# Plain fp32 products on the expert weights, in groups of 32 array columns, in place of three fp32r products on high and low parts

## The reference

```python
def ec_moe(h, w_router, w_gate, w_up, w_down):
    cap = CAPACITY_FACTOR * n // N_EXPERTS          # 64 of 512 latent tokens, 16 of 128 context tokens
    aff = jax.nn.softmax(logits, axis=-1)
    gate, idx = lax.top_k(jnp.swapaxes(aff, 1, 2), cap)
    xs = h[idx]                                     # per expert: 80 rows of 2048
    hid = silu(xs @ w_gate) * (xs @ w_up)           # w_gate, w_up: 2048 x 1024 per expert
    out = (hid @ w_down) * gate                     # w_down: 1024 x 2048 per expert
    return zeros.at[idx].add(out)
```

## Time and profile before

| | |
|---|---|
| median of three runs | 2361.98 us |
| profiled execution, its span (the page gives no other time for it) | 2364.1 us |
| expert stage, first to last matmul | 1235.8 to 2323.7 us |
| TensorE busy over the whole span | 2215.2 us, 94% |
| VectorE, ScalarE busy | 1512.7 us, 1202.5 us |
| expert weights | 384 transfers of 1 MB |

### The profile page before, as it was taken

The page is one execution under the profiler, slowest core; times in us unless marked ns, Lnnn a source line. Parts: engine busy times, 40 slices in busy tenths (PEclk is TensorE's granted clock), DMA queues, the critical chain, the costliest instruction groups (busy, mean ns, idle before and its releaser), DMA issues.

```text
span 2364.1 us, 28774 instructions
## 1 busy us (share of the span) xinstructions
PE 2215.2 (94%) x10944; PEld 1547.9 (65%) x10944; DVE 1512.7 (64%) x1577; ACT 1202.5 (51%) x1255; POOL 241.9 (10%) x97
## 2 busy tenths in 40 slices
PE   5899999999999997999929999999999999999993
PEld 3467777777877775788826666666666666666662
DVE  3242221233556665333268999999999999999994
ACT  4431221122246666112147777777776777777763
POOL 1010000001000000000000111211122222111211
PEclk8999999999999997999959999999999999999997
DMA  9875566654220003222389999999999999999995
GB/s 371 317 238 213 221 235 240 232 196 179 72 92 1 1 1 139 95 72 70 127 318 363 382 383 382 395 390 388 389 388 386 385 382 394 395 386 387 384 376 189
DMA packets 187519, 623.71 MB, mean 264 GB/s; under 512 B 10960, under 2 KB 12496, under 8 KB 156048
## 3 DMA queue, kind: packets, MB, share of 16 engines
q1 hardware_dynamic: 177328, 565.76, 63.0%
q0 software_dynamic: 6112, 35.40, 5.4%
q10 hardware_dynamic: 4000, 21.50, 2.3%
HBM read 593.08 MB, written 29.56 MB: 263 GB/s over the span
## 4 chain that ended last, share of the span: by engine, by line
PE 88%; DMA 5%; DVE 3%; ACT 1%; SPq 1%; issue 1%; POOL 0%; ACTq 0%; POOLq 0%; DVEq 0%
PE ps L560 25%; PE ps L561 24%; PE ps L562 24%; PE ps L809 3%; PE ps L755 3%; PE ps L843 3%; DMA arena<-in_w_mod 2%; PE ps L826 1%; PE ps L830 1%; PE ps L958 1%; DVE mx L1545 1%; DMA xn_d<-arena 1%; SPq L624 1%; PE ps L896 1%; PE ps L786 1%
## 5 line engine op out<-in xcount | busy, mean ns | idle before, releaser
L1748 DVE TENSOR_TENSOR E_w_lo<-arena,E_w_hi 128x2048 fp32r<-128x2048 f32 x384 | 871.2, 2286 | 88.5 <-ACT E_w_hi L1248 79.4
L1248 ACT ACTIVATE E_w_hi<-arena 128x2048 fp32r<-128x2048 f32 x380 | 728.8, 1918 | 277.0 <-PE ps L562 277.0
L560 PE MATMUL ps<-E_w_hi,E_xsT_hi 128*80 128x512 f32 x1024 | 404.6, 395 | 2.3 <-DVE E_xsT_lo L1741 2.3
L561 PE MATMUL ps<-E_w_hi,E_xsT_lo 128*80 128x512 f32 x1024 | 403.1, 394 | 0.0
L562 PE MATMUL ps<-E_w_lo,E_xsT_hi 128*80 128x512 f32 x1024 | 400.2, 391 | 0.0
L1528 DVE TENSOR_TENSOR B_w_lo<-arena,B_w_hi 128x1024 fp32r<-128x1024 f32 x72 | 87.6, 1224 | 369.3 <-ACT B_w_hi L1076 369.0
L560 PE MATMUL ps<-B_w_hi,B_x_hi 128*128 128x512 f32 x720 | 290.5, 403 | 1.6 <-DVE B_x_lo L1532 1.1
L561 PE MATMUL ps<-B_w_hi,B_x_lo 128*128 128x512 f32 x720 | 282.2, 392 | 0.0
L562 PE MATMUL ps<-B_w_lo,B_x_hi 128*128 128x512 f32 x720 | 281.7, 391 | 0.0
L1076 ACT ACTIVATE B_w_hi<-arena 128x1024 fp32r<-128x1024 f32 x72 | 75.6, 1058 | 338.9 <-DMA arena<-in_w_in 293.0
L1360 POOL DMA_INDIRECT acc_d<-arena,idxC x16 | 148.9, 9309 | 765.1 <-DVE arena L1792 765.1
(11 more groups left out here) (202 smaller groups left out, 2548.2 us busy)
## 6 DMA issues: line engine op xcount, KB each, us to landing
arena<-in_w_expert_gate SPq DMA_DIRECT2D x128, 1024.0 KB, 12.9
arena<-in_w_expert_up SPq DMA_DIRECT2D x128, 1024.0 KB, 12.5
arena<-in_w_expert_down SPq DMA_DIRECT2D x128, 1024.0 KB, 15.2
arena<-in_w_mod SPq DMA_DIRECT2D x64, 1024.0 KB, 6.4
arena<-in_w_in SPq DMA_DIRECT2D x36, 1024.0 KB, 5.0
arena<-in_w_mod SPq DMA_DIRECT2D x64, 512.0 KB, 9.7
arena<-in_w_out SPq DMA_DIRECT2D x16, 1024.0 KB, 5.3
acc_d<-arena POOLq DMA_DIRECT2D x1, 5120.0 KB, 30.2
```

The source lines that it names most:

```text
L560: eng.matmul(out, x_hi, w_hi, start=start, stop=False)
L561: eng.matmul(out, x_lo, w_hi, start=False, stop=False)
L1248: act.activation(split_e(j)[0][:, :], at(slot_e(j), D), ACT.Copy).then_inc(xw_hi, 1)
L1748: dve.tensor_tensor(w_lo[:, :], at(slot_e(j), D), w_hi[:, :].bitcast(F32), ALU.subtract).then_inc(xw_lo, 1)
```

## The change

The expert stage of TensorE is written anew; nothing before it changes.

- No high and low parts: the ScalarE copy and the VectorE subtraction of every chunk are gone, and so are those of the gathered and of the hidden rows. The slots of the high parts stay unused. TensorE waits for the landing of a chunk itself.
- The products are plain fp32. The chosen rows are kept in two blocks: `xL` (64 latent rows) and `xC` (16 context rows with 16 zero columns, 32 wide). A call of `latent_round` or `context_round` issues four matmuls, each 32 columns wide, into the four quarters of one PSUM bank. Two latent halves times two column blocks of 512 make a latent round; four column blocks of 512 make a context round. For each 128-row step of gate and up there are two latent rounds and one context round, for each down chunk the same: 16 x 3 + 8 x 3 = 72 rounds, 288 matmuls per expert.
- Chunks 0 to 15 now alternate gate and up, and the up chunk has the layout of the gate chunk: two pieces of 4 KB per partition in place of four of 2 KB.
- The hidden rows are laid out over all 128 partitions (latent) and 64 (context), transposed by four 128-wide and four 64-wide transposes in place of eight of 80 rows.
- At the end of an expert ScalarE copies the result out of PSUM in 6 pieces into the row buffer, then VectorE scales it there in one instruction of 80 x 2048.

```diff
-        wu_v = w_up.rearrange("o e (q i p) (h n) -> (o e) q h p i n", i=4, p=P, n=NB)
+        wu_v = w_up.rearrange("o e (q i p) n -> (o e) q p i n", i=2, p=P)
...
-                if j < 8:
-                    src = wg_v[bass.ds(e, 1), j].rearrange("e p i n -> (e p) i n")
+                if j < 16:
+                    src = (wg_v, wu_v)[j % 2][bass.ds(e, 1), j // 2].rearrange("e p i n -> (e p) i n")
...
-                    sp.wait_ge(xused, e * XCH + (HI_E + j - RING_E + 1))
+                    sp.wait_ge(xused, e * XCH + (j - RING_E + 1))
...
+            def latent_round(b, rows, w_pair, start, stop):
+                for q in range(4):
+                    mm = pe.matmul(bank(b)[32 * q:32 * q + 32, :], rows[:, 32 * (q % 2):32 * (q % 2) + 32], w_pair[q // 2],
+                                   start=start, stop=stop, skip_group_check=True)
+                return mm
+            def context_round(b, rows, w_four, start, stop):
+                for q in range(4):
+                    mm = pe.matmul(bank(b)[32 * q:32 * q + 32, :], rows, w_four[q], start=start, stop=stop,
+                                   skip_group_check=True)
...
             with pe.Fori(0, NE) as e:
-                for c in range(16):
-                    pe.wait_ge(xw_lo, e * XCH + (c + 1))
-                        mm = three_products(pe, bank(b)[0:CAP, :], (xsT_hi[:, k, :], xsT_lo[:, k, :]),
-                                            (w_hi[:, cs], w_lo[:, cs]), k == 0, k == KC - 1)
...
+                for i in range(6):
+                    latent_pair(e, i)
+                    context_pair(i, 0)
+                    context_pair(i, 1)
+                    if i == 3:
+                        pe.wait_ge(gathered, e * 16 + 32)
+                        pe.wait_ge(y_taken, e + 1)
+                        gathered_transposes(False)
+                latent_pair(e, 6)
+                latent_pair(e, 7).then_inc(lat_done, 1)
+                context_pair(6, 0)
+                context_pair(6, 1)
+                context_pair(7, 0)
+                pe.wait_ge(hid_ready, e * 2 + 1)
+                for b in range(4):
+                    mm = pe.transpose(bank(3)[:, P * b:P * (b + 1)], hidL[:, P * b:P * (b + 1)], ident[:, :])
+                context_pair(7, 1)
+                pe.wait_ge(hT_ready, e * 2 + 1)
...
+                act.wait_ge(lat_out, e + 1)
+                for h in range(2):
+                    act.activation(xrow_out[0:CL, 2 * NB * h:2 * NB * (h + 1)], bank(4, 2)[CL * h:CL * (h + 1), :], ACT.Copy)
+                act.wait_ge(xused, e * XCH + 24)
+                for n in range(4):
+                    ins = act.activation(xrow_out[CL:CAP, NB * n:NB * (n + 1)], bank(6)[CXP * n:CXP * n + CX, :], ACT.Copy)
+                ins.then_inc(y_taken, 1)
```

More of the change, by code:

```diff
@@ new lines, in _ @@
+                landed(e, 16)
+                latent_down(0, 0)
+                latent_down(0, 1)
+                landed(e, 17)
+                latent_down(1, 0)
+                pe.wait_ge(hid_ready, e * 2 + 2)
+                latent_down(1, 1)
+                for b in range(4):
+                    mm = pe.transpose(bank(7)[:, 2 * CXP * b:2 * CXP * (b + 1)], hidC[0:2 * CXP, P * b:P * (b + 1)],
+                                      ident[0:2 * CXP, 0:2 * CXP])
+                mm.then_inc(ht_done, 1)
@@ new lines, in _ @@
+                landed(e, 18)
+                latent_down(2, 0)
+                latent_down(2, 1)
+                pe.wait_ge(hT_ready, e * 2 + 2)
+                for f in range(3):
+                    context_down(f)
+                for f in range(3, 8):
+                    landed(e, 16 + f)
+                    latent_down(f, 0)
+                    mm = latent_down(f, 1)
+                    if f == 7:
+                        mm.then_inc(lat_out, 1)
+                    context_down(f)
@@ L1229, in rows_high @@
[L1229 to L1250 removed]
+            act.sem_inc(y_taken, 1)
@@ L1696, in _ @@
             groups = [(g, min(6, KC - 6 * g)) for g in range(3)]
-            def scale_rows():
-                for g, n in groups:
-                    src = bank(4 + g)[:, 0:n * CAP].rearrange("p (k c) -> p k c", k=n)
-                    for v, cs in kinds:
-                        ins = dve.tensor_tensor(xstage[:, 6 * g:6 * g + n, cs], src[:, :, cs],
-                                                bc(A2[:, v, 6 * g:6 * g + n], cs.stop - cs.start, 2), ALU.mult)
-                ins.then_inc(t1_scaled, 1)
@@ L1724, in first_sum @@
+            dve.memset(xC[:, :, :], 0.0).then_inc(xC_zero, 1)
+            dve.wait_ge(xC_zero, 1)
+            for g in range(3):
                 dve.wait_ge(t1_done, g + 1)
-                for v, cs in kinds:
-                    ins = dve.tensor_tensor(xstage[:, ks, cs], src[:, :, cs], bc(A2[:, v, ks], cs.stop - cs.start, 2), ALU.mult)
+                ins = scaled(g)
                 if g == 2:
@@ L1731, in first_sum @@
                     link(ins)
-                for v, cs in kinds:
-                    ins = dve.tensor_tensor(xstage[:, ks, cs], xstage[:, ks, cs], bc(modT[:, 3, v, ks], cs.stop - cs.start, 2),
-                                            ALU.add)
-                ins.then_inc(xsum_ready, 1)
-            def first_low(g):
-                ks = slice(6 * g, 6 * g + groups[g][1])
-                dve.wait_ge(xhi_ready, g + 1)
-                dve.tensor_tensor(xsT_lo[:, ks, :], xstage[:, ks, :], xsT_hi[:, ks, :].bitcast(F32), ALU.subtract)\
-                    .then_inc(xsT_ready, 1)
```

247 lines of the change are left out of this document (89 added, 158 removed).

## The result

The changed kernel takes 2332.11 us (median of four runs, 2331.4 to 2334.88). The kernel before, run beside it, takes 2361.15 us (2360.17 to 2363.41). The ratio is 0.9872, 95% interval [0.9859, 0.9884]: 29 us, 1.3% faster. The profiled execution has a span of 2330.0 us.

The account below looks back on a forecast made before the run. DMA transfers, already slower than TensorE, were taken to bound the expert stage: last landing 2288, TensorE's end 2294, plus 43.8 gives span 2338; 26.3 off the median 2361.98 gives 2335.7 us. Range 2316 to 2362, its own 2328 to 2345.

Parts of the forecast that it names:

- What binds: Expert stage before the change: DMA engines need 68.6 us per expert, TensorE 67.86; transfers live on the ring's lead.
- TensorE, 64.4 us per expert: TensorE's new expert work: 72 rounds at 0.855 us, transposes and mode changes, 64.4 us against 67.86.
- Up at the gate's rate: Up weight transfers in 4 KB pieces: 20.5 us per matrix for 21.7, 18 us over about 15 experts.
- Transfers at 67.4 us per expert: DMA in the expert stage: 68.6 less 1.2 us, with gather and adding write unchanged at 6.6; last landing 2288.
- Rival C: Gather and adding write disturb weight transfers less, half of 6.6 us gone; TensorE binds, about 2310 us; chance 0.08.
- The lead: Weight ring: 12 chunks loaded before the stage; TensorE uses up this lead in about ten experts, landing time near 30 us.
- From the last landing to TensorE's end: End of expert stage: TensorE's last product ends some 6 us (3 to 8) after the last chunk lands, at 2294.
- The tail: After TensorE's last product: ScalarE copies, then VectorE scaling, add 3.4 us; 40.4 us becomes 43.8.
- The sum: Whole kernel: last product at 2294, 43.8 us behind it, span 2338, 26 less; time 2335.7 us.
- Rival A: TensorE's sequencer can't feed 16 records per round; at 60 ns each the time is 2428 us; chance 0.14.
- Rival B: TensorE's bank and block changes cost up to 6.5 us per expert, making it the bound; 2340 to 2365; chance 0.14.
- The clock: TensorE in the expert stage: waits expected under 1 us at a time, so a falling clock is no separate case.

Follow-up runs that it names:

- experiments 1 and 2: Changed kernel without 5 of each expert's 24 context rounds: 2329.11 us; changed kernel without the adding writes of the first 15 experts: 2310.65 us.
- experiment 4: Changed kernel with up chunks in 2 KB pieces again: 2347.44 us; kernel before with only up chunks in 4 KB pieces: 2365.27 us.
- experiment 6: Changed kernel with eight extra VectorE subtractions of 128 x 1024 beside each expert's adding write: 2332.49 us, ratio 0.9866.
- experiment 7: Changed kernel with a weight ring of 16 slots for 12 and loops over pairs of experts: 2355.9 us; with 8 KB gate and up pieces too: 2356.63 us.

## Why the prediction was right, step by step

Forecast 2335.7, measured 2332.1; the mechanism was right, and two terms were mis-sized by a few us.

- **What binds.** The DMA engines "need 67.86 + 0.72 = 68.6 us per expert, more than TensorE does". Shown: experiments 1 and 2 from both sides, and 4, where before with faster up transfers keeps its time and loses its growing landing time (6.2 us in place of 17.3).
- **TensorE, 64.4 us per expert.** Measured 64.45, with and without traffic. The round of 0.855 us, read off two short runs in the mod stage, is 0.859 here over eight in a row.
- **Up at the gate's rate.** Right: 13 to 15 us of the gain (experiment 4), 18 forecast.
- **Transfers at 67.4 us per expert.** Measured 66.8. This is the term that was mis-sized: "Gather and adding write stay as they are", 6.6 us. They took 6.0, about 9 us over 15 experts, and that is the distance of the last landing, 2288 forecast and 2278.7 measured (chunk 12, the first behind the ring's lead, was issued at 1240.7 before and at 1240.0 after). Rival C had this mechanism, with half the 6.6 us; about a tenth came. Its reason, VectorE beside GpSimd, is not borne out by experiment 6 as far as that goes, and with 8 KB pieces the term is 6.6 again. A part of the 0.6 may be an error of reading: by its bytes an expert (25.2 MB of weights and 1.3 MB of gather and adding write, at 387 to 388 GB/s) needed 68.2 to 68.4 us before, not 68.6. Why the term moves between 5.9 and 6.6 us is open.
- **The lead.** "In about ten experts", and a landing time near 30 us. It was gone after six, with a landing time of 21 us. I counted twelve chunks of lead; gate and up slots come free only in pairs, behind six rounds, which takes part of it away (how much is not measured). It costs nothing by itself, since the end was that of the transfers in both cases.
- **From the last landing to TensorE's end.** 6 us forecast, 8.1 measured, at the upper end of its range of 3 to 8.
- **The tail.** 43.8 us forecast, 43.2 measured. VectorE ends its scaling at 2292.94, 6.2 us behind TensorE, as forecast.
- **The sum.** Transfers -9, lag +2, tail -1: the span was 2330.0 where 2338 was forecast, 8 less. Some 3 to 4 of these 8 us are not of the change. A run's time is 2 us above its own span in every other run on record, but the span of before that the forecast started from is 2 us above the median time: a late execution, which stored the sum ahead of the expert stage at 1186.92 us, where after stored it at 1183.88. From that store to the issue of chunk 12 it took 53.8 us, after 56.1, so the start of the transfers lost 2.3 us that the forecast had cancelling to within 2. Transfers that were too dear by 9 us were partly made up by a start and a lag that were too cheap by 2 us each; that the time came within 4 us (gain 29, forecast 26) is in part luck.

*Rival A* (sequencer) falls: 16 records in 0.859 us, 54 ns each, are sustained for whole experts. *Rival B* (changes of bank and block) falls: two rounds between two changes take 0.855 each, and an expert 64.45 for the 64.4 counted. *Rival C* is told above. That the loads of a round would show, as "TensorE: Matmul & The Clock Gate" of the Trainium skill has it (Part 3), is not what this trace shows either: in the window of 2146 to 2162 us the matmul records fill 16.00 of 16.00 us with 152 loads beside them. One load of 0.110 us laid bare in each half round would leave them at most 0.64 of the 0.859 us of a round. (The ends of matmul records are modelled.) *The clock* held: landing waits of TensorE of at most 1.6 us left it at 1.00; 3.8 us of standstill (experiment 7, granted 0.71 behind it) did not, and neither did a landing wait of 3.04 us in experiment 1 (0.86 from 2110 to 2118 us, 0.93 in the 8 us after).

## What to carry to other kernels

Where a ring lies between transfer and product, compare periods and not busy shares: a landing time that grows says that the transfers are already the slower side, whatever the waits say. The gain of a faster engine then ends at the next resource, and an edit that alone measures nothing (the layout) may carry half of the gain once the engine is faster. Times from different groups of runs are compared by the ratios to a kernel that ran beside each. Before a hot loop is lengthened or written out, ask where its instructions will come from.

## What the runs showed of the hardware

- Four fp32 matmuls of 128 x 512 on 32 columns each take 0.859 us together (64.45 us for 288 of them with 24 transposes), whether the queues move about 400 or 118 GB/s beside them.
- 1 MB transfers from DRAM ran at 387 GB/s with pieces of 2 KB per partition, at 407 to 410 with 4 KB and at 422 to 423 with 8 KB.
- One accumulating write of 80 x 8 KB rows per expert cost this kernel 21 us in all (23 by the ratios), without TensorE ever waiting for it.
- A loop body of two experts (about 150 KB of TensorE's instructions) cost 5.7 us a turn, where one of a single expert cost nothing; written out without a loop the code cost 15 to 16 us in the whole, at the weights' expense.
- GpSimd's indirect DMA instruction took 9.83 us in the kernel before, 1.43 after, and 2.16 after with VectorE subtracting beside it; the step from 1.43 to 2.16 did not show in the time.
